# Column panels of the mixing layers in half panels, with 512 moving columns

## The reference

```python
h = _rmsnorm(x, norm_mix[l])
z = h @ w_in[l]
(q_n, kc, vc, ks, vs, kw, vw, g_n, q_r, k_r, v_r, g_r, c_a, c_b, m_g) = _split_cols(z)
o_nsa = _nsa(q_n, kc, vc, ks, vs, kw, vw, g_n, ...)
o_ret = _retention(q_r, k_r, v_r, g_r, ret_gn[l])
o_conv = _conv_module(c_a, c_b, conv_w[l], ...)      # c_a * sigmoid(c_b), then 31 taps per channel
```

## Time and profile before

| | us |
|---|---|
| median of 3 runs | 1145.68 (1145.44 to 1145.97) |
| the profiled execution | 1145.91, span 1144.1 |
| PE busy | 1134.6 (99%) |
| PE weight loads busy | 949.7 (83%) |
| DVE busy | 823.8 (72%) |
| ACT busy | 587.5 (51%) |
| L1041, L1042, L1043 busy | 72.6, 72.4, 72.5 |
| L1066, L1069 (feed-forward, wide and narrow) busy | 129.9, 72.6 |

### The profile page before, as it was taken

How to read it: one execution, slowest core, us unless ns; L and a number is a source line. 1 busy time by engine, 2 the same in 40 slices (tenths; PEclk the granted TensorE clock), 3 DMA queues, 4 the chain that set the end, 5 groups by cost and what they waited for, 6 DMA issues and landing times.

```text
span 1144.1 us, 15970 instructions
## 1 busy us (share of the span) xinstructions
PE 1134.6 (99%) x6208; PEld 949.7 (83%) x6208; DVE 823.8 (72%) x1253; ACT 587.5 (51%) x742; POOL 140.2 (12%) x152
## 2 busy tenths in 40 slices
PE   9999999999999999999999999999999999999997
PEld 7888777788997777888888888997777888888886
DVE  6665666567699899787777454699899786777443
ACT  7555566544525676534455333426676534555332
POOL 1321232100003234000000000003234000000000
PEclk9999999999999999999999999999999999999999
DMA  9645535367545678654555655445677654555641
GB/s 360 233 177 194 217 146 183 121 231 258 169 149 211 190 213 221 184 183 156 213 184 186 217 199 195 168 160 201 190 207 221 186 182 167 201 188 190 223 154 38
DMA packets 35180, 219.35 MB, mean 192 GB/s; under 512 B 3872, under 2 KB 5408, under 8 KB 10784
## 3 DMA queue, kind: packets, MB, share of 16 engines
q1 hardware_dynamic: 33232, 205.72, 51.1%
q0 software_dynamic: 1728, 12.58, 5.9%
q10 hardware_dynamic: 144, 0.01, 0.0%
HBM read 217.25 MB, written 1.05 MB: 191 GB/s over the span
## 4 chain that ended last, share of the span: by engine, by line
PE 78%; issue 15%; DVE 3%; DVEq 1%; ACT 1%; DMA 1%; POOL 0%; POOLq 0%; SPq 0%; ACTq 0%
PE panel L992 31%; PE panel L998 16%; PE panel L1066 5%; PE panel L958 5%; PE tile L1080 4%; PE panel L1069 3%; PE panel L1043 3%; PE panel L1042 3%; PE panel L1041 3%; DVE area L2297 2%; PE heads_out L1283 1%; PE tile L1344 1%; PE heads_out L1430 1%; DMA area<-in_first_chunks_dram 1%; DVEq L2298 1%
## 5 line engine op out<-in xcount | busy, mean ns | idle before, releaser
L650 DVE TENSOR_TENSOR ring_parts<-ring,ring_parts 128x2048 fp32r<-128x2048 f32 (+1 forms) x170 | 387.4, 2283 | 154.5 <-ACT ring_parts L606 151.0
L606 ACT ACTIVATE ring_parts<-ring 128x2048 fp32r<-128x2048 f32 (+1 forms) x182 | 344.9, 1898 | 255.3 <-PE panel L998 187.7
L992 PE MATMUL panel<-ring_parts,hT 128*128 128x512 f32 (+1 forms) x1184 | 291.6, 392 | 0.0
L992 PEld LDWEIGHTS panel<-ring_parts,hT 128*128 128x128 f32 x1184 | 212.7, 188 | 47.9 <-issue 7.2
L992 PE MATMUL panel<-ring_parts,area_parts 128*128 128x512 f32 x736 | 177.4, 389 | 0.0
L992 PEld LDWEIGHTS panel<-ring_parts,area_parts 128*128 128x128 f32 x736 | 137.9, 188 | 28.5
L998 PE MATMUL panel<-ring_parts,hT 128*128 128x512 f32 (+1 forms) x592 | 151.0, 390 | 0.0
L1066 PE MATMUL panel<-hT,ring_parts 128*128 128x512 f32 x512 | 129.9, 393 | 0.0
L998 PEld LDWEIGHTS panel<-ring_parts,hT 128*128 128x128 f32 x592 | 107.4, 188 | 23.3 <-issue 2.5
L2297 DVE SCALAR_TENSOR_TENSOR area<-area,cw 128x256 f32<-128x256 f32 x240 | 105.0, 499 | 2.8
L1066 PEld LDWEIGHTS panel<-hT,ring_parts 128*128 128x128 f32 x512 | 91.6, 189 | 16.0
(11 more groups left out here) (255 smaller groups left out, 1231.7 us busy)
## 6 DMA issues: line engine op xcount, KB each, us to landing
ring<-in_w_layers_dram SPq DMA_DIRECT2D x140, 1024.0 KB, 4.9
ring<-in_w_first_dram SPq DMA_DIRECT2D x38, 1024.0 KB, 5.0
ring_parts<-in_w_layers_dram POOLq DMA_DIRECT2D x12, 1024.0 KB, 8.7
area<-in_second_bias_dram SPq DMA_DIRECT2D x8, 320.0 KB, 3.2
ring<-in_w_layers_dram SPq DMA_DIRECT2D x4, 560.0 KB, 3.9
ring<-in_w_first_dram SPq DMA_DIRECT2D x4, 512.0 KB, 9.5
area<-in_first_bias_dram SPq DMA_DIRECT2D x4, 384.0 KB, 4.4
area<-in_later_bias_dram SPq DMA_DIRECT2D x1, 1536.0 KB, 12.1
```

The source lines that it names most:

```text
L606: act.activation(ring_lo[:, SLOTS + hi, 0:w], ring[:, slot, 0:w], ACT.Copy).then_inc(high_ready, 1)
L650: g.tensor_tensor(ring_lo[:, slot, 0:w], ring[:, slot, 0:w], ring_lo[:, SLOTS + hi, 0:w], ALU.subtract).then_inc(low_ready, 1)
L992: pe.matmul(ps[:, b, 0:width], t[:, 4 * i + k, b * P:(b + 1) * P], hi[:, k, :], start=(i == k == 0 and t is of[0]), stop=False)
```

## The change

The four panels become eight half panels (cb0, cb1, ca0, ..., q1), each with a panel buffer of its own, computed by `wide_columns_out` as the feed-forward panels are. The second half of each bank, the product of the high weights with the low activations, has to be added to the first. ScalarE copies it to a new buffer `cross` in SBUF, which holds two half panels; VectorE adds the first half to it there, which frees the PSUM buffer, and takes its operand from `cross` instead of from PSUM.

```diff
-LAYER_PANELS = (["gr", "cb", "ca", "k4", "q", "vsg", "qkr", "vr", "mg0", "mg1", "mg2", "mg3",
+COLUMN_PANELS = [f"{p}{j}" for p in ("cb", "ca", "k4", "q") for j in range(2)]
+LAYER_PANELS = (["gr", *COLUMN_PANELS, "vsg", "qkr", "vr", "mg0", "mg1", "mg2", "mg3",
...
+AREA_2["cross"] = within("L", 0, 1024)
...
-            def columns_out(part, name):
...
-            def wide_columns_out(part, i, groups=1, before_last=None, after={}):
+            def wide_columns_out(part, panels, groups=1, before_last=None, after={}):
...
                 for p in ("cb", "ca", "k4", "q"):
-                    columns_out(part, p)
+                    wide_columns_out(part, p)
...
                         if u == 0:
-                            for p in ("q", "k4"):
-                                bp, before = part.turn("panel", p)
-                                pe.wait_ge(panel_evicted[bp], before * 2 + 2)
+                            pe.wait_ge(columns_stored, l + 1)
```

ScalarE:

```diff
-                round_after(act, part, "gr/1", "cb/0")
+                cross = two("cross").rearrange("p (s m t) -> p s m t", s=2, m=2)
+
+                def keep_columns(name):
+
+                    i = COLUMN_PANELS.index(name)
+                    ps = panel_of(act, part, name)
+                    if i + 8 * l >= 2:
+                        act.wait_ge(columns_taken, l * 8 + i - 1)
+                    act.activation(cross[:, i % 2], ps[:, :, TOKENS:2 * TOKENS], ACT.Copy).then_inc(columns_kept, 1)
+                    round_after(act, part, f"{name[:-1]}/{name[-1]}")
+
+                round_after(act, part, "gr/1")
+                keep_columns("cb0")
+                keep_columns("cb1")
                 act.wait_ge(conv_gate_in, l + 1)
                 act.activation(two("tz"), two("tz"), ACT.Tanh, scale=0.5).then_inc(conv_gate, 1)
-                round_after(act, part, "cb/1", "ca/0", "ca/1", "k4/0", "k4/1", "q/0", "q/1", "vsg/0")
+                for name in COLUMN_PANELS[2:]:
+                    keep_columns(name)
+                round_after(act, part, "vsg/0")
```

VectorE:

```diff
-                lows_to(part, "cb/0")
+                def columns(name):
+
+                    i = COLUMN_PANELS.index(name)
+                    ps, whole = panel_of(v, part, name), cross[:, i % 2]
+                    v.wait_ge(columns_kept, l * 8 + i + 1)
+                    v.tensor_tensor(whole, whole, ps[:, :, 0:TOKENS], ALU.add).then_inc(panel_sem(part, name), 2)
+                    v.drain()
+                    return whole
...
                 for b in range(NB):
-                    e = v.tensor_tensor(tz2[:, b], ps[:, b, :].rearrange("p (c t) -> p c t", c=2), R2, ALU.mult)
-                    e.then_inc(panel_sem(part, "cb"), 1)
+                    v.tensor_tensor(tz2[:, b], columns(f"cb{b}"), R2, ALU.mult).then_inc(columns_taken, 1)
+                    if b == 0:
+                        lows_to(part, "cb/0")
...
-                lows_to(part, "ca/0")
-                ps = panel_of(v, part, "ca")
                 for b in range(NB):
-                    v.tensor_tensor(u_all[:, 2 * b:2 * b + 2, 32:288], tz2[:, b], ps[:, b, :].rearrange("p (c t) -> p c t", c=2),
-                                    ALU.mult).then_inc(panel_sem(part, "ca"), 1)
+                    v.tensor_tensor(u_all[:, 2 * b:2 * b + 2, 32:288], tz2[:, b], columns(f"ca{b}"), ALU.mult).then_inc(columns_taken, 1)
+                    if b == 0:
+                        lows_to(part, "ca/0")
...
                 lows_to(part, "ca/1")
                 taps(0, 4)
-                lows_to(part, "k4/0")
...
+                kc = columns("k40")
...
-                        v.tensor_tensor(kcP[0:HD, i, g, :], ps[rows, 0, s:s + TOKENS], R[rows, :], ALU.mult)
-                        e = v.tensor_tensor(kcP[HD:P, i, g, 0:TOKENS - 1], ps[rows, 0, s + 1:s + TOKENS], R[rows, 1:TOKENS], ALU.mult)
-                e.then_inc(panel_sem(part, "k4"), 1)
+                        v.tensor_tensor(kcP[0:HD, i, g, :], kc[rows, i, :], R[rows, :], ALU.mult)
+                        e = v.tensor_tensor(kcP[HD:P, i, g, 0:TOKENS - 1], kc[rows, i, 1:TOKENS], R[rows, 1:TOKENS], ALU.mult)
+                e.then_inc(columns_taken, 1)
+                lows_to(part, "k4/0")
+                v.tensor_tensor(two("kT").rearrange("p (i t) -> p i t", i=2), columns("k41"), R2, ALU.mult).then_inc(columns_taken, 1)
                 v.drain()
                 lows_to(part, "k4/1")
...
-                lows_to(part, "q/0")
...
                 for b in range(NB):
-                    v.scalar_tensor_tensor(qT[:, b], ps[:, b, :].rearrange("p (c t) -> p c t", c=2), HD ** -0.5, R2, ALU.mult, ALU.mult)\
-                     .then_inc(panel_sem(part, "q"), 1)
+                    v.scalar_tensor_tensor(qT[:, b], columns(f"q{b}"), HD ** -0.5, R2, ALU.mult, ALU.mult).then_inc(columns_taken, 1)
+                    if b == 0:
+                        lows_to(part, "q/0")
+                v.drain().then_inc(columns_stored, 1)
                 lows_to(part, "q/1")
                 taps(4, EARLY_TAPS)
```

More of the change, by code:

```diff
@@ L86, in halves_of @@
             continue
-        if p.startswith("ff"):
+        if p.startswith("ff") or p in COLUMN_PANELS:
             out.append((f"{p[:-1]}/{p[-1]}", p))
@@ L474, in block_kernel @@
         hid_kept = sem("hidden_products_kept")
+        columns_kept = sem("cross_products_of_column_panel_kept")
+        columns_taken = sem("column_panel_taken_on")
+        columns_stored = sem("queries_and_keys_stored")
         conv_gate_in = sem("conv_gate_argument_ready")
@@ L1054, in wide_columns_out @@
                     for j in range(2):
-                        name = f"ff{i}{j}"
+                        name = f"{panels}{j}"
                         if group == 0:
@@ L1060, in wide_columns_out @@
                             ps, done = panel[b], panel_done[b]
-                        hi, lo = (w.rearrange("p (k n) -> p k n", k=KC) for w in wait_parts(part, f"ff{i}/{j}"))
+                        hi, lo = (w.rearrange("p (k n) -> p k n", k=KC) for w in wait_parts(part, f"{panels}/{j}"))
                         for m in range(2):
@@ L1517, in _ @@
                 columns_ready(part, "z", 0)
-                wide_columns_out(part, 0, 2, lambda: columns_ready(part, "z", 1), {b: lambda b=b: turn_last(b) for b in range(NB)})
+                wide_columns_out(part, "ff0", 2, lambda: columns_ready(part, "z", 1), {b: lambda b=b: turn_last(b) for b in range(NB)})
                 for i in range(1, FF_PANELS):
-                    wide_columns_out(part, i)
+                    wide_columns_out(part, f"ff{i}")
                 for c in range(2):
@@ L2268, in _ @@
                 R2 = R.unsqueeze(1).broadcast_to([P, 2, TOKENS])
-                lows_to(part, "cb/0")
+                cross = two("cross").rearrange("p (s m t) -> p s m t", s=2, m=2)
+                def columns(name):
[5 more added lines that the diff above has]
+                    return whole
                 tz2 = two("tz").rearrange("p (b c t) -> p b c t", b=2, c=2)
-                ps = panel_of(v, part, "cb")
                 for b in range(NB):
-                    e = v.tensor_tensor(tz2[:, b], ps[:, b, :].rearrange("p (c t) -> p c t", c=2), R2, ALU.mult)
-                    e.then_inc(panel_sem(part, "cb"), 1)
+                    v.tensor_tensor(tz2[:, b], columns(f"cb{b}"), R2, ALU.mult).then_inc(columns_taken, 1)
+                    if b == 0:
+                        lows_to(part, "cb/0")
                 v.drain().then_inc(conv_gate_in, 1)
@@ L2302, in _ @@
                 taps(0, 4)
-                lows_to(part, "k4/0")
-                ps = panel_of(v, part, "k4")
-                v.tensor_tensor(two("kT").rearrange("p (i t) -> p i t", i=2), ps[:, 1, :].rearrange("p (i t) -> p i t", i=2), R2, ALU.mult)\
-                 .then_inc(panel_sem(part, "k4"), 1)
+                kc = columns("k40")
                 kcP = two("kcP").rearrange("p (i g t) -> p i g t", i=2, g=2)
@@ L2309, in _ @@
                     for g in range(2):
-                        s = i * TOKENS
                         rows = slice(HD * g, HD * g + HD)
-                        v.tensor_tensor(kcP[0:HD, i, g, :], ps[rows, 0, s:s + TOKENS], R[rows, :], ALU.mult)
-                        e = v.tensor_tensor(kcP[HD:P, i, g, 0:TOKENS - 1], ps[rows, 0, s + 1:s + TOKENS], R[rows, 1:TOKENS], ALU.mult)
-                e.then_inc(panel_sem(part, "k4"), 1)
+                        v.tensor_tensor(kcP[0:HD, i, g, :], kc[rows, i, :], R[rows, :], ALU.mult)
[3 more added lines that the diff above has]
+                v.tensor_tensor(two("kT").rearrange("p (i t) -> p i t", i=2), columns("k41"), R2, ALU.mult).then_inc(columns_taken, 1)
                 v.drain()
@@ L2333, in _ @@
                 v.tensor_tensor(blk_parts[:, :, 1, :], whole, blk_parts[:, :, 0, :], ALU.subtract).then_inc(blocks_ready, 1)
-                lows_to(part, "q/0")
                 qT = two("qT").rearrange("p (b c t) -> p b c t", b=2, c=2)
```

(7 more changed lines are left out.)

## The result

The changed kernel takes 1150.13 us (median of 6 runs, 1149.95 to 1150.68), the kernel before 1145.63 us on the same chip. The ratio is 1.0038, 95% interval 1.0028 to 1.0049: +4.5 us where +3.4 was forecast, slower, as forecast. The profiled execution has a span of 1148.4 us, 4.3 us more than before.

What follows compares the result with a forecast made beforehand. TensorE, busy 1134.6 of 1144.1 us, was taken to bound the kernel. Its 1.39 us saved a layer against 3.1 us of stalls on VectorE's queue gave +1.7 a layer, +3.4 us: 1149.1 us, range 1145.3 to 1152.0.

Steps and rivals of the forecast that it cites:

- TensorE's work: Column panels cb to q: 16 groups of 2.793 us, 44.69 us in place of 46.08, saving 1.39 us a layer.
- The additions and the buffers: Column stage: VectorE's eight additions of 0.75 us, 6.0 us a layer; half buffers must be emptied within 5.59 us, not 11.5.
- The schedule by hand: Layer 1, VectorE's queue from q/0's low part: stalls before q0, q1 and vsg of 0.9, 0.9, 1.2 us; vsg 1.7 us later.
- The second layer the same: Layer 2's column stage has the same rows, shifted by 427.89 us: +1.7 us again, +3.4 us in all.
- The moved low part: Each first half's low part comes behind the first addition: hidden in early waits, counted above in late ones.
- What is late next: First logits and attention: logits 2.9 us later, VectorE's further 1.2 us of lag taken up by its waits: 0.
- rival C: Attention: VectorE's 1.2 us of lag is left there and paid once more, 1151.5 us; 13%.
- Bounds: Addition with its waits 0.60 to 1.20 us, kcP from SBUF 0 to 0.8 us less over eight: 1146.8 to 1152 us.
- B: Column stage: kcP quicker from SBUF, drains cost little, stalls about eat the gain: 1145 to 1148 us, middle 1146.8; 25%.
- The prediction's A: Column stage: half buffers never hold TensorE up, its gain comes through: -1.4 us a layer, 1142.9 us; 9%.

Runs made afterwards that it cites:

- kernel 5: As 1 (no additions, ScalarE frees the buffer), with q/1's low part back ahead of the kcP multiplications: 1142.69 us.
- 7: Against the changed kernel: ScalarE copies both halves and frees the PSUM buffer, VectorE adds in SBUF: 1150.93 us.
- 2: Against the changed kernel: no additions, ScalarE only copies, VectorE frees each buffer where its addition stood: 1147.43 us.
- 6: Against the changed kernel: only q/1's low part moved back ahead of the kcP multiplications: 1150.09 us.
- 1: Against the changed kernel: no additions on VectorE, ScalarE copies the first half and frees the buffer itself: 1144.91 us.
- 8: Against the changed kernel: one tap ahead of k40's addition instead of four, one between q0 and q1, four behind q1: 1150.79 us.
- 9: Against 8: two of the taps moved on into the attention, to where VectorE used to wait: 1148.3 us.

## Why the prediction was right, and the 1.1 us that it missed

**TensorE's work** (16 groups of 2.793 us): right. The pitch is in the trace, and kernel 5 has the gain by itself, -3.2 us for -2.8 (interval -4.4 to -1.8 us), 1.38 us a layer in the stage. The pitch rule of the Trainium skill ("TensorE: Matmul & The Clock Gate", section Back-to-back issue gap) would have given an estimated 0.6 us for two layers, which the trace and this interval exclude. The prediction used the rule as one for a stream; the page gives it for a product by itself and says that a stream of weight loads and products keeps another pace.

**The additions and the buffers**: right for the changed kernel, where all three waits end with an addition that frees a buffer. Beyond it the two are not equal. Without additions it is 1147.43 us, with free buffers 1150.93, without both 1144.91, and 1142.69 with the low part moved back. So the longer queue on VectorE is the loss, and the half buffers are the place where TensorE meets it first: with them out of the way (7) the next things that VectorE hands over are late instead, and nothing is gained. The half buffers cost by themselves only where VectorE's old order already holds one too long (2: 0.36 and 0.54 us a layer).

**The schedule by hand**: right in place and order, too small in size. Per layer it said +1.7 us. From the stage's first product to the end of vsg's first sixteen products it is 2.18 us: 342.81 + 2.33 - 294.58 = 50.56, where before it was 340.63 + 2.22 - 294.47 = 48.38. The term that was mis-sized is the vsg start. VectorE's queue to q0's addition was 342.08 - 319.65 = 22.43 us for 22.16 forecast. Of the 0.27 us, 0.10 lie between the first tap and the first addition (6.81 us for 6.71), 0.18 in kT's multiplication, which now has a drain right behind it (0.78 us to the next start, 0.60 before), and 0.04 in the additions; kcP takes 0.06 less. The queue began at 319.65 instead of 319.6. The first products after a wait cost 0.11 us more (2.33 for 2.22). And I had read vsg's old start off the chain of waits, 340.79, which counts from the end of the product before it; its record starts at 340.63. That is 0.16 us. Against these stand 0.11 us by which the whole stage began later than in the trace before. Together 0.48 us a layer, 1.0 of the 1.1 us.

**The second layer the same**: right, 48.00 and 47.99 us.

**The moved low part, costed at nothing**: right for this kernel (6), but not harmless. It is the next wait, 0.88 us a layer in 1 and 2.09 us in 7. By the forecast's own sum it was ready at 335.0 (k41 emptied at 335.7, less the addition), against the 334.8 at which q1 wanted it, and the forecast did not name it among the next late.

**What is late next, 0**: right for the changed kernel. It has no wait for the logits, and from vsg to layer 2's row-scale product it takes 381.59 us for 381.36, of which 0.11 are vsg's first products. The wait of 0.31 us in layer 2 is gone, since TensorE comes later itself. But the forecast took the wrong step for TensorE's nearest need. It named the turn at 360.59, with 2.8 us to spare; the second pair of scores comes first, at 353.46 before the change, and takes over a tile whose logits VectorE reads from 350.85 to 351.48, some 2 us ahead. It binds in 7 and 8. So rival C's mechanism is real: in 7, 8 and 9, where TensorE comes less late or not at all, the lag is paid in the attention. TensorE's timeline of the kernel before:

```profile
353.46 0.49 PE L1450 MATMUL tile<-area 64*128 64x128 f32 x4
```

**Bounds**: kcP from SBUF was hardly quicker (0.43 us apart), so B's ground fell away. The prediction's A would have needed 3.1 us less on VectorE, which nothing gave. The bounds 1146.8 and 1152 are counted from the profiled 1145.91 us, the forecast from the median; from the median they are 1146.6 and 1151.8. The measured time lies between them either way.

## What to carry to other kernels

When TensorE gets faster by giving part of the sum to another engine, look at that engine's timeline where the work will stand, not at its share: 9.7 idle us of 46 lay in the first half, where they took the additions of cb and ca, and were worth nothing to k4 and q. Apply such a change panel by panel: the half with room gained 2 us, the half without cost 5 us, and the two don't add. Freeing the buffer sooner, or moving work within the same queue, only moves the wait (7, 8). Moving work into a wait of a busy engine pays only if nobody waits for what stands next in its order (9).

## What was not expected of the hardware

- A wait costs TensorE more than its length. Between the last group before it and the one behind it, 327.24 + 0.95 should have been the next start and 329.41 was it, 1.22 us, and the eight products behind it take 2.11 us for 2.00: 1.33 us for a wait recorded as 1.06.
- After waits of TensorE of 1.1 us the granted clock was still 1.00. One of 3.00 us was followed by 0.50 in one layer and not in the other, one of 3.36 us by 0.50 in both. Why it held in the one layer is open.
- GpSimd's addition of 128x512 in SBUF took 1.30 us, where 1.0 was expected from its 1.47 us for 128x768. Of the twelve tap instructions of VectorE that ran beside two such additions, the longest took 1.53 us instead of 0.48.
